# The first microseconds of a two-block transformer kernel: first weight panel loaded by ScalarE, input in 512 KB loads, ten discarded products

## The reference

```python
def rms_norm(x, g):
    xf = x.astype(jnp.float32)
    y = xf * lax.rsqrt(jnp.mean(xf * xf, axis=-1, keepdims=True) + EPS)
    return (y * g.astype(jnp.float32)).astype(x.dtype)

def first_block(x, mem, norm_mix_g, w_in, ...):
    h = x
    for _ in range(DEPTH):
        h = h + parallel_mixer(rms_norm(h, norm_mix_g), w_in, ...)
        h = h + memory_cross_attention(rms_norm(h, norm_xattn_g), ...)
        u = jax.nn.relu(rms_norm(h, norm_mlp_g) @ mlp_w1)
        h = h + (u * u) @ mlp_w2
    return h

def parallel_mixer(xn, w_in, ...):
    proj = xn @ w_in
    fq, fk, fv, ff, gq, gk, gv, glr, gr = jnp.split(proj, _split_points(), axis=-1)
    ...
```

## Time and profile before

| | us |
|---|---|
| three runs | 2126.83, 2127.73, 2128.53 |
| median | 2127.73 |
| the profiled execution | 2127.39 |
| its span, first to last instruction | 2125.6 |
| outside the span | 1.8 |
| PE busy in the span | 2113.5 |

### The profile page before, as it was taken

The page is one execution under the profiler, slowest core; times in us unless marked ns, Lnnn a source line. Parts: engine busy times, 40 slices in busy tenths (PEclk is TensorE's granted clock), DMA queues, the critical chain, the costliest instruction groups (busy, mean ns, idle before and its releaser), DMA issues.

```text
span 2125.6 us, 28548 instructions
## 1 busy us (share of the span) xinstructions
PE 2113.5 (99%) x11590; PEld 1745.0 (82%) x11590; DVE 1187.5 (56%) x2068; ACT 912.6 (43%) x1555; POOL 0.2 (0%) x4
## 2 busy tenths in 40 slices
PE   8999999999999999999999999999999999999999
PEld 6778888888888888888888888887777888888887
DVE  5856676543443454344356787757885465434345
ACT  6765446432232332222234566646775243222224
POOL 0000000000000000000000000000000000000000
PEclk9999999999999999999999999999999999999999
DMA  5122531233333332323324623221112323333321
GB/s 191 60 80 79 200 99 60 64 101 94 99 99 99 99 97 92 97 91 99 99 80 136 204 86 94 86 85 51 46 31 80 119 81 99 99 99 99 99 90 70
DMA packets 186165, 203.71 MB, mean 96 GB/s; under 512 B 6945, under 2 KB 175154, under 8 KB 185522
## 3 DMA queue, kind: packets, MB, share of 16 engines
q1 hardware_dynamic: 186034, 201.89, 30.1%
HBM read 190.86 MB, written 4.19 MB: 92 GB/s over the span
## 4 chain that ended last, share of the span: by engine, by line
PE 97%; DVE 1%; ACT 1%; DMA 0%; issue 0%; SPq 0%; DVEq 0%; ACTq 0%
PE lin L602 28%; PE lin L604 28%; PE lin L603 28%; PE turned L728 3%; PE score L824 3%; PE mix L838 2%; PE mix L1314 1%; PE score L956 1%; DMA raw<-in_w_in_dram 0%; PE score L602 0%; ACT wh L1497 0%; PE score L603 0%; PE score L604 0%; PE mix L602 0%; PE mix L1325 0%
## 5 line engine op out<-in xcount | busy, mean ns | idle before, releaser
L602 PE MATMUL lin<-xh,wh 128*128 128x512 f32 (+1 forms) x1478 | 579.9, 392 | 3.3 <-DVE xl L2357 3.0
L604 PE MATMUL lin<-xh,wl 128*128 128x512 f32 (+1 forms) x1478 | 569.5, 385 | 0.0
L603 PE MATMUL lin<-xl,wh 128*128 128x512 f32 (+1 forms) x1478 | 568.5, 385 | 0.0
L602 PE MATMUL lin<-ah,wh 128*128 128x512 f32 x1044 | 407.2, 390 | 0.2 <-DVE h L2392 0.2
L604 PE MATMUL lin<-ah,wl 128*128 128x512 f32 x1044 | 405.8, 389 | 0.0
L603 PE MATMUL lin<-al,wh 128*128 128x512 f32 x1044 | 405.6, 389 | 0.0
L2325 DVE TENSOR_TENSOR wl<-raw,wh 128x2048 fp32r<-128x2048 f32 x128 | 293.4, 2292 | 156.1 <-ACT wh L1487 156.1
L1487 ACT ACTIVATE wh<-raw 128x2048 fp32r<-128x2048 f32 x128 | 244.0, 1906 | 271.9 <-PE lin L604 271.9
L602 PEld LDWEIGHTS lin<-xh,wh 128*128 128x128 f32 x1478 | 278.4, 188 | 61.6 <-issue 5.6
L604 PEld LDWEIGHTS lin<-xh,wl 128*128 128x128 f32 x1478 | 278.1, 188 | 56.4
L603 PEld LDWEIGHTS lin<-xl,wh 128*128 128x128 f32 x1478 | 278.7, 189 | 51.6 <-issue 0.2
(11 more groups left out here) (391 smaller groups left out, 2171.1 us busy)
## 6 DMA issues: line engine op xcount, KB each, us to landing
raw<-in_ffn_w_dram SPq DMA_DIRECT2D x60, 1024.0 KB, 5.3
raw<-in_w_in_dram SPq DMA_DIRECT2D x38, 1024.0 KB, 5.3
raw<-in_mlp_w_dram SPq DMA_DIRECT2D x32, 1024.0 KB, 5.3
raw<-in_xattn_wkv_dram SPq DMA_DIRECT2D x8, 1024.0 KB, 5.3
raw<-in_w_out_dram SPq DMA_DIRECT2D x8, 1024.0 KB, 5.2
arena<-arena SPq DMA_DIRECT2D x104, 64.0 KB, 2.1
raw<-in_ffn_w_dram SPq DMA_DIRECT2D x8, 768.0 KB, 4.5
raw<-in_xattn_wq_dram SPq DMA_DIRECT2D x4, 1024.0 KB, 5.1
```

The costliest lines, as they stand in the source:

```text
L602: nc.tensor.matmul(o, w[0], x[0], start=first, stop=False)
L603: nc.tensor.matmul(o, w[0], x[1], start=False, stop=False)
L604: return nc.tensor.matmul(o, w[1], x[0], start=False, stop=last)
```

## The change

- SP now issues the gains and then the input in four loads of 512 KB (tiles 0 and 1, 2 and 3, 4 and 5, 6 and 7), all with rows of 4 KB. It no longer issues `first` and `small`.
- ACT issues three DMAs as its first instructions: the k-tiles 0 to 3 of `first` (512 KB, rows of 4 KB), `small`, and the k-tiles 4 to 7 of `first` (512 KB).
- After them ACT copies one column of the gains to the scratch tile `idle`; this ACTIVATE needs only the gains, and the table load stands ahead of it.
- ACT makes the high parts of both input tiles 0 and 1 before the first part of the panel; the parts 0, 1, the small columns and part 2 follow in a row, part 3 follows input tile 3. DVE's order follows.
- PE multiplies the gains ten times instead of four, into another bank (`score0`), and takes the panel's k-tiles 0 and 1 before the first two small tiles.

```diff
-        ld_x = [sem("ld_x" + str(n)) for n in range(5)]
-        X_LOAD = [0, 1, 2, 2, 3, 3, 4, 4]
+        ld_x = [sem("ld_x" + str(n)) for n in range(4)]
+        X_LOAD = [0, 0, 1, 1, 2, 2, 3, 3]
...
-            f = P0["fqk"] % 2
-            input_tiles(0)
-            sp.dma_start(raw[:, f, 0:2, :], d["first"][:, 0:2]).then_inc(ld_f, 16)
-            sp.dma_start(sm_raw, d["small"]).then_inc(raw_in[0], 16)
-            input_tiles(1, 2)
-            sp.dma_start(raw[:, f, 2:KT, :], d["first"][:, 2:KT]).then_inc(raw_in[f], 16)
-            input_tiles(3, 4)
+            input_tiles(0, 1, 2, 3)
...
             def discarded(n):
 
                 for _ in range(n):
-                    nc.tensor.matmul(pl[0][0:NROWS, 0:NROWS], gT[:], gT[:], start=True, stop=True)
+                    nc.tensor.matmul(ps[0][0:NROWS, 0:NROWS], gT[:], gT[:], start=True, stop=True)
 
             pe.wait_ge(ld_gain, 16)
-            discarded(4)
+            discarded(10)
...
             for c in range(2):
                 begin(f, c)
                 first_tile(c, 0)
+            pe.wait_ge(nm_lo, 2)
+            pe.wait_ge(f_lo, 2)
+            for c in range(2):
+                first_tile(c, 1)
             pe.wait_ge(conv_done, p + 1)
             small_tile(0)
             small_tile(1)
-            pe.wait_ge(f_lo, 2)
-            for c in range(2):
-                first_tile(c, 1)
             for k in range(2, 6):
                 small_tile(k)
...
+            act.dma_start(raw[:, f % 2, HALVES[0], :], d["first"][:, HALVES[0]]).then_inc(ld_f, 16)
+            act.dma_start(sm_raw, d["small"]).then_inc(raw_in[0], 16)
+            act.dma_start(raw[:, f % 2, HALVES[1], :], d["first"][:, HALVES[1]]).then_inc(raw_in[f % 2], 16)
             act.wait_ge(ld_gain, 16)
+            nc.scalar.activation(idle[:, 0:1], gT[:, 0:1], ACT.Copy)
             for k in range(KT):
                 act.wait_ge(ld_x[X_LOAD[k]], 16)
                 high("mix", "norm_mix_g", k)
-                if k == 0:
+                if k == 1:
                     act.wait_ge(ld_f, 16)
                     part_hi(f, F_PARTS[0], f_hi)
+                    part_hi(f, F_PARTS[1], f_hi)
                     conv_small()
-                elif k == 1:
-                    part_hi(f, F_PARTS[1], f_hi)
+                    part_hi(f, F_PARTS[2], f_hi)
                 elif k == 3:
                     act.wait_ge(raw_in[f % 2], landed(f))
-                    part_hi(f, F_PARTS[2], f_hi)
-                elif k == 5:
                     part_hi(f, F_PARTS[3], hi_done)
...
                 if k == 0:
                     dve.wait_ge(f_hi, 1)
                     part_lo(f, F_PARTS[0], f_lo)
-                    dve.wait_ge(hi_done, 1)
-                    nc.vector.tensor_tensor(sm_l, sm_raw.rearrange("p (k n) -> p k n", k=KT), sm_h.bitcast(F32), ALU.subtract).then_inc(conv_done, 1)
                 elif k == 1:
                     dve.wait_ge(f_hi, 2)
                     part_lo(f, F_PARTS[1], f_lo)
-                elif k == 3:
+                    dve.wait_ge(hi_done, 1)
+                    nc.vector.tensor_tensor(sm_l, sm_raw.rearrange("p (k n) -> p k n", k=KT), sm_h.bitcast(F32), ALU.subtract).then_inc(conv_done, 1)
                     dve.wait_ge(f_hi, 3)
                     part_lo(f, F_PARTS[2], f_lo)
-                elif k == 5:
+                elif k == 3:
                     dve.wait_ge(hi_done, f + 1)
                     part_lo(f, F_PARTS[3], conv_done)
```

## The result

| | before | after |
|---|---|---|
| median, us (22 runs each on the same chips) | 2127.77 | 2130.36 |
| lowest and highest run | 2126.64, 2129.12 | 2129.26, 2133.28 |
| the profiled execution | 2127.39 | 2131.88 |
| its span | 2125.6 | 2130.1 |

The ratio is 1.0013, 95% interval 1.0007 to 1.0019. (Slow executions are left out of all ratios here; there was one, of 4483 us, of the kernel before in b_again.) The changed kernel is slower by 2.6 us (0.12%): within the 0.2% that the prediction called no change, but 4.0 us above the forecast and 1.1 above the upper end of its range.

A forecast was written before the change was run, and what follows sets the result against it. PE was taken as the bound, busy 2113.5 of 2125.6 us. A first dense product 1.67 us later, less 2.66 us of low clock, made -0.99 us: 2127.39 became 2126.4, range 2125.2 to 2129.3.

The forecast's parts named there:

- The bound, and the shift carried to the end: Whole kernel: PE bounds it, 97% of the chain, so a shift of the second panel's begin shifts the end equally.
- The table load: ACT at the start: the load leaves the path, ending at 3.4 us; worth 1.28 us against the old landing.
- The landing: First input and panel loads at the start: in at 6.8 us, 1.35 us after the old begin at 5.44.
- if the queues share them evenly, both land together: First input load and panel half on two queues: both land when 1.11 MB, plus other bytes, have moved.
- the 0.35 MB on top: Other bytes moved before the landing, taken from a range of 0.16 to 0.6 MB; landing at 1.46 MB moved.
- L: Time at which the first large loads land: 6.8 us, bounds 6.0 and 7.75, at about 300 GB/s.
- rival 2: Start's slow pace not made by load size: landing 7.75, first dense product 10.1, clock high, 2127.3 us; chance 0.15.
- From landing to first product: ACT, DVE, then PE at the start: first dense product 2.35 us after the landing, against 2.04 before.
- S: Start of PE's first dense product: forecast 9.15 us, 1.67 us later than 7.48.
- No new wait behind S: PE from first dense product to second panel: no wait; later tiles and panel halves arrive in time, cover about 1.1 us.
- The discarded products: PE before dense work: ten at 0.47 us end at 7.3, rest 1.85 us, all 2.66 us of low clock come back.
- Rival 1: PE's clock rises late all the same: 2127.7 to 2129.1 us, centre 2128.4; chance 0.27.

The follow-up runs named there:

- b_again: The kernel before, unchanged, run once more with a profile; median -0.22 us against before, ratio 0.9999.
- a_disc22: The changed kernel with 22 discarded products in place of 10; median +1.47 us against before, ratio 1.0009.
- a_again: The changed kernel, unchanged, run once more with a profile; median +2.70 us against before, ratio 1.0013.
- a_disc4: The changed kernel with 4 discarded products in place of 10; median +3.14 us against before, ratio 1.0015.
- a_one_queue: The changed kernel with ACT's three loads moved back to SP, between the input loads, sizes kept; median -1.18 us against before, ratio 0.9997.
- b_table: The kernel before with only the early table load added (copy of one gains column); median -0.80 us against before, ratio 0.9998.
- b_table_actq: The kernel before with the table load early and the panel's and small columns' loads, in old sizes, issued by ACT; +0.51 us against before, ratio 1.0003.
- b_bank: The kernel before with its four discarded products put into bank score0 instead of lin0; median -0.13 us against before, ratio 0.9999.
- a_hold: The changed kernel with SP issuing the three later input loads only when the first has landed; median +2.98 us against before, ratio 1.0013.
- a_bank: The changed kernel with its ten discarded products put into the old bank, lin0; median +3.04 us against before, ratio 1.0013.
- a_act_hold: The changed kernel with ACT holding the small columns and second panel half until the first input load landed; +2.69 us against before, ratio 1.0013.

## Why the prediction was wrong

The steps in the prediction's order.

*The bound, and the shift carried to the end*: right. PE stays at 99%. In the profiled executions the span less the second panel's start is 2098.7 before, 2098.6 in b_again and a_disc22, 2099.3 in a_again, a_disc4 and a_one_queue; only after (2101.5, the wait until 1210 us) and b_table (2100.6, where PE waits 1.4 us near 251 us) stand out.

*The table load*: right. ACT's issues took 0.38 to 0.45 us each, and the load ended at 3.52 (forecast 3.4).

*The landing*: this is the step that failed, **8.1 us and not 6.8**, of which the failed term is "if the queues share them evenly, both land together", with the 0.35 MB on top. The queues did not finish evenly: the load issued first landed 2.2 us ahead, and 0.64 MB of other bytes had gone by when the other one was in, at 8.12 us. Before had 0.61 MB by the same account when its second input tile landed, the upper end of my own 0.16 to 0.6, so taking the middle was the choice that was wrong. The sum itself has a slip as well: 1.25 MB at the 300 GB/s that I took from 3.0 us on are 4.2 us, so L should have read 7.2; 6.8 needs 329 GB/s. The pace up to the landing was then right in the mean (299 GB/s), slower at first (252) and faster later, so that 1.46 MB were in at 7.45. Of the 1.3 us, the slip is thus 0.4, the slow beginning 0.3, and the bytes that moved beyond 1.46 MB before the input was in, 0.29 MB, are 0.7. With rival 2's landing at 7.75 the error would have been 0.4. All three errors leaned the same way.

The Trainium skill, DMA: Bandwidth & Descriptors, Rules for kernel authors, has it that several issuing engines bring no bandwidth, since their loads interleave on the same 16 engines. What the prediction read from it, that the panel's bytes hold up the input's, came true at both sizes. On the bandwidth the traces agree at the large sizes, 218 GB/s to 8.21 us with two queues and 227 with one (a_one_queue), and not at the old ones, 243 with two (b_table_actq) and 201 with one (b_table), each in one execution and for the start alone; there the measurement decides. In its section on queues, rings and completion order it says that an engine takes the queues with work in turn, a packet from each. No run here shows packets in turn; the landings show that equal loads on two queues still finish 2.2 us apart.

*From landing to first product*: 2.19 us where 2.35 were forecast. With the landing, S is 10.31, +2.83 us in place of +1.67.

*No new wait behind S*: right. PE doesn't wait from 10.31 to 28.63. ACT converted the second panel's first half from 22.35 on and DVE was done with it at 24.7, long before it was needed.

*The discarded products*: wrong in two terms. Their price: 0.47 us a product was 1.89 us over four, which counts the last one's tail; ten took 4.22. They began later too, because the gains landed at 3.20 in place of 2.58, and still ended at 7.42 (forecast 7.3). Their effect: with S at 10.31 the rest was 2.89 us and not 1.85. The clock had risen and fell at 11.1, 0.8 us after work resumed. The low clock then cost 8 x 0.2 us, some 1.6 (a_disc22 shows 1.56); before it cost 2.66. So 1.0 us came back, neither all of it nor nothing. Sum: +2.83 - 1.0 = +1.8, measured 1.76. Against before's three executions (S 7.66, ten slow, 26.45 in the mean) it is +2.7 - 0.4 = +2.2.

The forecast that the discarded work would raise the clock was right, though with luck in its yardstick: it set 4.7 us against 5.3 us of dense work, which the 13 slow products make 5.7, and in b_again and b_bank the clock rose after 4.4 and 3.1. Whether the forecast rest of 1.85 us would have kept it high no run shows, but it lies nearer to those that did: rests of 0.5 us (a_disc22) and 1.55 us (a_one_queue) kept it high, rests of 2.5 (a_hold), 2.9 (after, a_again, a_bank) and 3.1 us (a_act_hold) did not. Rival 1 named the mechanism and priced it from 2127.7 to 2129.1, but with the forecast's landing. The case that came was rival 2's landing and rival 1's clock at once, and I had priced each alone. They hang together: a late landing lengthens the rest, and the rest is what lets the clock fall. By my own terms both together give 2127.39 + 2.6 = 2130.0 if no clock comes back, and 2128.7 if half does; the first is outside the range I gave.

## What to carry to other kernels

Give the operand that the first instruction waits for a queue position with nothing beside it or ahead of it: a second issuing engine saved issue time (0.4 us a load here) but shares the same DMA engines, and with its own load issued first it delayed the awaited load from 4.2 to 6.1 us at 256 KB and from 4.9 to 8.1 at 512 KB. Work that is there to warm TensorE should last until close to the real work (here a rest of 1.55 us kept the high clock and one of 2.5 us did not), so fix its length only once the landing is known, and add up the two errors (late operand, cooled clock) as one case.

## What the runs showed of the hardware that was not expected

- Two equal 512 KB loads on two queues, issued 0.3 us apart, landed 5.0 and 6.9 us after their issue.
- The first microseconds are slow in all forms: 225 to 324 GB/s from 3.0 to 6.5 us, with rows of 2 KB or 4 KB, against 413 from 7 to 12 us. Neither the size of the rows nor the number of queues sets the value alone: a single queue has 242 with small loads and 301 with large ones, two queues have 324 with small and 252 with large. Here b_table, b_table_actq and a_one_queue, in turn, one execution each:

```profile
3.00:6.50 3.50, 1.54 (x8) 1.26 (x7) 0.75 (x1) 0.96 (x2) 0.00 (x0) 1.00 0.83 242
```

```profile
3.00:6.50 3.50, 1.90 (x8) 1.62 (x8) 0.00 (x0) 1.18 (x3) 0.00 (x0) 1.00 0.96 324
```

```profile
3.00:6.50 3.50, 3.50 (x20) 3.34 (x19) 0.71 (x1) 1.33 (x2) 0.00 (x0) 1.00 0.96 301
```

- The clock fell 0.8 us after dense work had resumed (0.4 in a_again, 1.2 in a_bank), with 2.9 us of rest behind it; behind 3.1 us of rest (a_act_hold) it was low from the first dense product on. So a first few products at full pace don't say that the rest was harmless.
- The granted clock's column reads 1.00 while the clock has not yet risen at all, as in before and in a_disc4, where products 0.43 us apart stand beside it; it reads 0.50 only after a fall.
